# Latent attention: the rough scores, past-key products and turned maxima of a pair of heads moved to other steps

## The reference

```python
def mla_latent(h, w_in, q_norm, kv_norm, w_uq, w_uk, w_uv, w_out, ckv_ctx, kpe_ctx):
    ...
    q_lat = jnp.concatenate([q_nope, axial_rope(q_pe)], axis=-1)
    k_lat = jnp.concatenate([k_nope, bcast_heads(axial_rope(k_pe))], axis=-1)
    q_ctx = jnp.concatenate([q_nope, q_pe], axis=-1)
    k_ctx = jnp.concatenate([kc_nope, bcast_heads(kpe_ctx)], axis=-1)
    o = joint_attention([q_lat, q_ctx], [k_lat, k_ctx], [v, vc], MLA_SCALE)
    return merge_heads(o) @ w_out
```

## Time and profile before

| | us |
|---|---|
| median of 3 runs | 1739.69 |
| the profiled execution | 1740.12 |
| its span | 1738.3 |
| PE busy | 1674.2 (96%) |
| DVE busy | 1102.8 (63%) |
| ACT busy | 735.0 (42%) |
| POOL busy | 213.5 (12%) |

### The profile page before, as it was taken

How to read it: one execution, slowest core, us unless ns; L and a number is a source line. 1 busy time by engine, 2 the same in 40 slices (tenths; PEclk the granted TensorE clock), 3 DMA queues, 4 the chain that set the end, 5 groups by cost and what they waited for, 6 DMA issues and landing times.

```text
span 1738.3 us, 26413 instructions
## 1 busy us (share of the span) xinstructions
PE 1674.2 (96%) x10650; PEld 1494.3 (86%) x10650; DVE 1102.8 (63%) x1726; ACT 735.0 (42%) x1238; POOL 213.5 (12%) x204
## 2 busy tenths in 40 slices
PE   5999999899999999999999999999999999999997
PEld 3999864689999999999989974445999999999996
DVE  3777666856757777785587647886585653332345
ACT  3433235755653312213345745654475332221333
POOL 0000014432100000000120402443310000000011
PEclk7999999999999999999999989999999999999998
DMA  9455212131556456473412500002154722222231
GB/s 334 155 174 166 82 47 61 29 104 31 149 176 176 121 170 194 122 205 99 116 38 49 149 13 1 1 1 83 52 146 134 206 74 73 73 74 80 79 85 61
DMA packets 266794, 181.63 MB, mean 104 GB/s; under 512 B 26237, under 2 KB 239090, under 8 KB 265650
## 3 DMA queue, kind: packets, MB, share of 16 engines
q1 hardware_dynamic: 266674, 179.96, 35.7%
HBM read 173.75 MB, written 3.62 MB: 102 GB/s over the span
## 4 chain that ended last, share of the span: by engine, by line
PE 81%; DVE 9%; ACT 3%; issue 3%; DMA 2%; SPq 1%; POOL 0%; DVEq 0%; ACTq 0%; POOLq 0%
PE ps L824 21%; PE ps L826 21%; PE ps L825 21%; PE ps L1397 3%; PE ps L1407 2%; DMA ada_a<-in_w_ada 1%; PE ps L990 1%; PE ps L992 1%; PE ps L991 1%; DVE w_lo L575 1%; PE ps L1024 1%; PE ps L1006 1%; PE ps L878 1%; ACT km L1923 1%; ACT w_hi L566 1%
## 5 line engine op out<-in xcount | busy, mean ns | idle before, releaser
L566 ACT ACTIVATE w_hi<-stage 128x1024 fp32r<-128x1024 f32 (+1 forms) x176 | 184.7, 1052 | 615.8 <-PE ps L826 500.1
L575 DVE TENSOR_TENSOR w_lo<-stage,w_hi 128x1024 fp32r<-128x1024 f32 (+1 forms) x176 | 216.8, 1233 | 281.9 <-ACT w_hi L566 281.7
L824 PE MATMUL ps<-hM_hi,w_lo 128*128 128x320 f32 x952 | 295.2, 310 | 0.0
L826 PE MATMUL ps<-hM_hi,w_hi 128*128 128x320 f32 x952 | 294.2, 309 | 0.0
L825 PE MATMUL ps<-hM_lo,w_hi 128*128 128x320 f32 x952 | 294.1, 309 | 0.0
L824 PE MATMUL ps<-h_hi,w_lo 128*128 128x320 f32 x824 | 255.9, 311 | 2.6 <-DVE h_lo L2497 2.6
L826 PE MATMUL ps<-h_hi,w_hi 128*128 128x320 f32 x824 | 254.6, 309 | 0.0
L825 PE MATMUL ps<-h_lo,w_hi 128*128 128x320 f32 x824 | 254.6, 309 | 0.0
L2742 POOL TENSOR_TENSOR rstd<-rstd,sq 128x320 f32<-128x320 f32 x73 | 77.3, 1064 | 960.8 <-ACT sq L1490 959.2
L824 PEld LDWEIGHTS ps<-hM_hi,w_lo 128*128 128x128 f32 x952 | 178.7, 188 | 3.4 <-issue 3.4
L825 PEld LDWEIGHTS ps<-hM_lo,w_hi 128*128 128x128 f32 x952 | 178.7, 188 | 0.1
(11 more groups left out here) (412 smaller groups left out, 3525.8 us busy)
## 6 DMA issues: line engine op xcount, KB each, us to landing
stage<-in_w_mlp_out SPq DMA_DIRECT2D x83, 512.0 KB, 4.2
stage<-in_w_mlp_in SPq DMA_DIRECT2D x80, 512.0 KB, 4.6
slab_mlp<-in_w_ada SPq DMA_DIRECT2D x28, 1024.0 KB, 5.3
stage<-in_w_in_ac SPq DMA_DIRECT2D x28, 512.0 KB, 3.9
slab_ac<-in_w_ada SPq DMA_DIRECT2D x12, 1024.0 KB, 6.1
ada_a<-in_w_ada SPq DMA_DIRECT2D x8, 1024.0 KB, 16.6
stage<-in_w_out_ac SPq DMA_DIRECT2D x8, 512.0 KB, 4.1
stage<-in_w_out_c SPq DMA_DIRECT2D x8, 512.0 KB, 4.3
```

What stands on the lines that cost most here:

```text
L566: nc.scalar.activation(hi_place(n)[:, 0:width], stage[:, n % STAGE, 0:width], ACT.Copy)\
L575: nc.vector.tensor_tensor(lo_place(n)[:, 0:width], stage[:, n % STAGE, 0:width], hi_place(n)[:, 0:width].bitcast(F32), ALU.subtract).then_ ...
L824: mm(out, lo[:, k], xh, start=j == 0, stop=False)
L826: last = mm(out, hi[:, k], xh, start=False, stop=j == k_tiles - 1)
```

## The change

`ROUGH_AT` says at which steps a rough score is issued (pairs ahead, number 0 to 7). Before, steps 0 to 5, 8 and 9 have one, and steps 6 and 7 none. Now steps 2 and 5 have none. Three instead of two rough scores stand before the loop. The past products move from steps 1 and 5 to 0 and 6, the turned maxima (and ACT's copies of them) from 3 and 7 to 2 and 8, ACT's second `rounded_head` from step 8 to 7, and DVE's four late sums from steps 0, 2, 3, 4 to 0, 1, 2, 3.

```diff
-ROUGH_AT = {0: (1, 2), 1: (1, 3), 2: (1, 4), 3: (1, 5), 4: (1, 6), 5: (1, 7), 8: (2, 0), 9: (2, 1)}
+ROUGH_AT = {0: (1, 3), 1: (1, 4), 3: (1, 5), 4: (1, 6), 6: (1, 7), 7: (2, 0), 8: (2, 1), 9: (2, 2)}
+PAST_AT, ROWS_AT = (0, 6), (2, 8)
...
             rough_scores(1, 0, 0)
             rough_scores(1, 0, 1)
+            rough_scores(1, 0, 2)
...
-                    if p < MLA_PAIRS - 1 and i in (1, 5):
-                        rough_past(p + 1, i // 5)
-                    if p < MLA_PAIRS - 1 and i in (3, 7):
-                        latent_rows(p + 1, i // 7)
+                    if p < MLA_PAIRS - 1 and i in PAST_AT:
+                        rough_past(p + 1, PAST_AT.index(i))
+                    if p < MLA_PAIRS - 1 and i in ROWS_AT:
+                        latent_rows(p + 1, ROWS_AT.index(i))
...
-                    if p < MLA_PAIRS - 1 and i in (3, 7):
-                        latent_row(p + 1, i // 7)
-                    if p < MLA_PAIRS - 2 and i in (4, 8):
-                        rounded_head(p + 2, i // 8)
+                    if p < MLA_PAIRS - 1 and i in ROWS_AT:
+                        latent_row(p + 1, ROWS_AT.index(i))
+                    if p < MLA_PAIRS - 2 and i in (4, 7):
+                        rounded_head(p + 2, i // 7)
...
-            for j in range(2):
+            for j in range(3):
                 latent_peak(1, j)
...
-                    if p < MLA_PAIRS - 1 and i in (1, 5):
-                        past_peak(p + 1, i // 5)
+                    if p < MLA_PAIRS - 1 and i in PAST_AT:
+                        past_peak(p + 1, PAST_AT.index(i))
...
-                    if p and i in (0, 2, 3, 4):
-                        late_sums(p - 1, *{0: (0, 0), 2: (0, 1), 3: (1, 0), 4: (1, 1)}[i])
+                    if p and i < 4:
+                        late_sums(p - 1, i // 2, i % 2)
```

## The result

| | kernel before | changed kernel |
|---|---|---|
| median us | 1739.5 (7 runs, 1737.84 to 1740.97) | 1745.01 (7 runs, 1741.54 to 1747.11) |
| profiled execution us | 1740.12 | 1741.54 |

The changed kernel takes 1.0034 times as long, 95% interval 1.0023 to 1.0044: 5.9 us more (4.0 to 7.7), which is slower, by a third of a percent. The 5.9 us follow from the ratio; the two medians lie 5.5 us apart. The forecast was 1743.1 us with a range of 1735.5 to 1746.

The account below looks back on a forecast made before the run. PE was taken to bound the kernel, needing 17.95 us a pair, plus waits. From the profiled 1740.12 us, +1.3 + 0.8 + 1.6 - 0.3 gave 1743.5, or 1743.1 in terms of the median; range 1735.5 to 1746.

Parts of the forecast that it names:

- Term 1: Pairs 1 to 5: ACT's exponential of step 3 comes late behind the maxima copies, PE waits, 0.71 us a pair.
- Term 2: Pairs 2 to 5: `weight_sums` waits for DVE's last late sum, held by POOL; 19.43 us against 19.04, +1.6 us in all.
- rival (a): DVE wins the race for the last late sum, which ends at 8.2; pairs 18.7 us, total 1740.1 us; chance 0.24.
- Rival (c): Waits feed each other through late reciprocals; pairs 19.9 us, total 1745 to 1746; chance 0.16 with a longer slow clock included.
- Term 3: Pairs 1 and 6: pair 1 takes 18.7 us against 17.89, +0.8; pair 6 takes 17.8 against 18.14, -0.3.
- Term 4: Pair 0: PE's stall moves to the rough score of step 4, with the lower clock behind it, +1.3 us.

Follow-up runs that it names:

- e9: Changed kernel, POOL's copies ahead of `pair_low`, ACT's maxima copies one exponential later, first early sum after all four late sums: ratio 0.9960, run again 0.9976.
- e2: Changed kernel with ACT's copies of the turned maxima behind the exponential of step 3, not step 2: 1744.89 us, ratio 1.0031 to the kernel before.
- e3: Changed kernel with POOL's copies ahead of `pair_low` and ACT's maxima copies behind the exponential of step 3: 1737.15 us, ratio 0.9983 to the kernel before.
- e1: Changed kernel with POOL's two plain-query copies ahead of `pair_low`, not behind it: 1737.18 us, ratio 0.9989 to the kernel before.
- e7: Changed kernel with the four late sums moved back to steps 0, 2, 3 and 4: 1745.72 us, ratio 1.0036 to the kernel before.
- e8: Changed kernel with POOL's first early sum waiting for all four late sums, not two: 1737.22 us, ratio 0.9986 to the kernel before.

## Why the prediction was right, and where it was not

**What bounds the kernel.** Held. PE's own need of 17.95 us a pair was measured as 17.96 in e9.

**Term 1, ACT between steps 2 and 3.** Held: pair 1 took 18.71 us where 18.7 stood, and 17.96 in e2 without the wait, a cost of 0.75 where 0.71 was predicted.

**Term 2, the last late sum.** The mechanism was right: a DVE addition with two inputs in SBUF stands still while POOL works, `weight_sums` waits for it, and more of PE's work lies behind that point (10.43 + 9.0 = 19.43 predicted; the last sum was 0.7 us later, and the pair too). Its size was wrong: 4 x 1.10 us in place of 4 x 0.39. The step that failed is "POOL's two copies and the third late sum then take turns". They did not: all that POOL had ready, both copies and the early sum, went ahead of the third sum, which ended 8.82 us into the pair, not at 7.05. The fallback, "if both copies go ahead of the third sum the result is nearly the same", left out the early sum, which was ready by then as well. The race I saw between the last sum and the early sum was already lost one sum earlier, so rival (a) had no ground.

Rival (c) came nearest in number, with pairs of 19.9 us and a total of 1745 to 1746. Its mechanism was not what happened: it needed DVE to be free later than 2.2 us into a pair, and `pair_scaled` ended at 1.35 us (row below). Nor did pair 1 lose the 1.3 us that it has there.

```profile
1121.96 0.69 DVE L2675 TENSOR_TENSOR qm<-ps,nt 128x512 f32<-128x512 f32 x1
```

The Trainium skill's rule in "SBUF — State Buffer", section "Who interferes with whom", that whoever issues first holds the shared port for the whole instruction and the other blocks fully, fits these rows in one half: a held late sum ended 0.55 us after the POOL instruction, and a held copy 0.46 to 0.47 us after the late sum. The order does not follow from it. By the starts of the records the third late sum came first, 0.5 us before the second copy, and yet the copy was not held. That order was what the size hung on.

**Term 3.** Pair 1 +0.82 (0.8 predicted), pair 6 -0.43 (-0.3).

**Term 4, pair 0.** In the profiled execution wrong in sign, by little: from the peak of rough score (1, 1) to its end pair 0 took 22.82 us where it took 23.16, -0.3 and not +1.3. It ended at 1062.30, which is 1065.38 with the 3.08 us that this execution was ahead, just above the 1065 below which I called myself wrong. The wait for the rough score of step 4 was there, 1.87 us long, but the clock was low before it and not behind it. Windows of the changed kernel:

```profile
1040.00:1044.00 4.00, 3.69 (x9) 2.46 (x10) 1.71 (x4) 0.60 (x1) 0.61 (x1) 0.57 0.00 0
1044.00:1048.00 4.00, 4.00 (x10) 1.85 (x10) 3.97 (x7) 0.92 (x2) 0.61 (x1) 0.57 0.00 0
1048.00:1052.00 4.00, 2.13 (x6) 0.81 (x6) 3.93 (x6) 3.90 (x8) 2.56 (x3) 1.00 0.00 0
1052.00:1056.00 4.00, 4.00 (x14) 1.34 (x14) 2.74 (x4) 1.64 (x3) 2.51 (x3) 1.00 0.02 4
```

In e2 and e3, with the same order on PE and DVE in pair 0, it came as forecast. There the clock was 1.00 up to a stall of 3.41 us before the same rough score, and 0.50 behind it (e2, PE and a window):

```profile
1053.85 0.76 PE L1304 MATMUL ps<-w_hi,w_lo 128*128 128x512 f32 x1 [3.41 <-DVE w_lo L2623]
```

```profile
1054.00:1058.00 4.00, 4.00 (x7) 1.19 (x9) 2.76 (x4) 1.22 (x2) 0.97 (x1) 0.50 0.00 0
```

From the same peak on, pair 0 took 1.6 us more than before in both. In the other six executions with this order (changed, e1, e7, e8 and both of e9) it took 0.2 to 1.0 us less. So the mechanism is real, and the mistake was to count on it in every execution.

**The sum.** By the traces pairs 1 to 6 cost 4.78 us more and pair 0 0.34 less, together 4.4 where 3.4 was predicted, against 5.9 (4.0 to 7.7) measured. The rest lies within the interval. That the sum came so near is in part luck: term 2 was 2.8 us too small and term 4 1.6 us too large, and the two errors offset each other.

## What to carry to other kernels

When DVE additions with two inputs in SBUF stand still while POOL works, count how many POOL instructions are ready in a row where the addition arrives. An addition that finishes earlier can release the very instruction that then blocks the next one. Here a wait that holds that instruction back, or moving two copies that nothing was waiting for, gained 1.4 us a pair. A stall that hides under another shows its price only when the other is gone, so try the cures singly and together.

## What the runs showed that I had not expected

- The order between DVE and POOL. A DVE addition that waited under `pair_low` got in ahead of a copy behind it (2.02 us, ended 0.55 us after `pair_low`). The next addition had both copies and the early sum go ahead of it when all were ready (2.88 us), but got in between the two copies when the early sum was held back (1.09 us in e8), though its record starts 0.54 us after the first copy's in both. Why the readiness of an instruction two places further back matters is not settled.
- Where the low clock falls differs from execution to execution of the same program text: by 3.1 us of time ahead of the loop between the two profiled executions, and by 2 us in pair 0 between e1 and e2, which are alike there on PE and DVE. For differences of that size a total says little here, and the lengths of the pairs say much.
